# Raising the weight forms' buffers by 192 bytes, and splitting the MLP's plain weight chunks two at a time

## What is computed

```python
D_MODEL = 2048; SEQ = 256; DEPTH = 2; D_FF = 4 * D_MODEL
for l in range(DEPTH):
    ...                                   # mixer: input projection, branches, output projection
    x = layer_norm(ALPHA * x + mix, ln_mix_g[l], ln_mix_b[l])
    h = jnp.square(jax.nn.relu(x @ mlp_w1[l])) @ mlp_w2[l]
    x = layer_norm(ALPHA * x + h, ln_mlp_g[l], ln_mlp_b[l])
```

## Time and profile before

| | |
|---|---|
| median of 3 runs | 2216.68 us (2210.5 to 2217.85) |
| the profiled execution | 2210.79 us, of which the profiled span is 2209.1 us |
| TensorE (matmul) busy | 2187.7 us, 99% of the span |
| TensorE (weight load) busy | 2033.3 us, 92% |
| VectorE busy | 1665.5 us, 75% |
| ScalarE busy | 1152.0 us, 52% |
| chain that ended last | PE 90%, DVE 5%, issue 2%, ACT 2%, DMA 1% |
| mean granted TensorE clock | 0.997 of full speed |
| DMA | 190 GB/s over the span, its main queue 58.7% of 16 engines |

### The profile page before, as it was taken

The page is one execution under the profiler, slowest core; times in us unless marked ns, Lnnn a source line. Parts: engine busy times, 40 slices in busy tenths (PEclk is TensorE's granted clock), DMA queues, the critical chain, the costliest instruction groups (busy, mean ns, idle before and its releaser), DMA issues.

```text
span 2209.1 us, 36685 instructions
## 1 busy us (share of the span) xinstructions
PE 2187.7 (99%) x15395; PEld 2033.3 (92%) x15395; DVE 1665.5 (75%) x1942; ACT 1152.0 (52%) x1244; POOL 48.5 (2%) x77
## 2 busy tenths in 40 slices
PE   9999999999999999999999999999999999999998
PEld 9998988899999999899889999988989989999996
DVE  5999986977787688688765455568777777877786
ACT  5555584455555456466434444444555554555552
POOL 2000010000000000000100000000000000000000
PEclk9999999999999999999999999999999999999999
DMA  7555656555665666566846555564665666656674
GB/s 259 175 161 152 183 161 191 183 179 187 196 200 191 201 196 215 171 192 210 261 139 205 177 172 172 175 206 154 196 194 185 206 191 194 198 188 205 190 230 151
DMA packets 213237, 419.29 MB, mean 190 GB/s; under 512 B 12809, under 2 KB 13377, under 8 KB 212176
## 3 DMA queue, kind: packets, MB, share of 16 engines
q1 hardware_dynamic: 210832, 406.37, 58.7%
q0 software_dynamic: 1952, 10.04, 1.4%
q10 hardware_dynamic: 288, 0.52, 0.1%
HBM read 414.79 MB, written 2.10 MB: 189 GB/s over the span
## 4 chain that ended last, share of the span: by engine, by line
PE 90%; DVE 5%; issue 2%; ACT 2%; DMA 1%; DVEq 0%; SPq 0%; ACTq 0%
PE gemm L1653 13%; PE gemm L1655 13%; PE gemm L1656 13%; PE gemm L1629 12%; PE gemm L1631 12%; PE gemm L1630 11%; PE pair L2077 4%; PE pair L2081 4%; PE pair L2079 4%; DMA raw<-in_mlp_w 1%; PE pair L1810 1%; DVE lnp L1304 1%; DVE w_lo L1012 1%; ACT w_hi L677 1%; DVE w_lo L1482 1%
## 5 line engine op out<-in xcount | busy, mean ns | idle before, releaser
L1012 DVE TENSOR_TENSOR w_lo<-raw,w_hi 128x1024 fp32r<-128x1024 f32 x656 | 787.6, 1226 | 289.7 <-ACT w_hi L677 283.6
L677 ACT ACTIVATE w_hi<-raw 128x1024 fp32r<-128x1024 f32 x656 | 681.8, 1056 | 578.0 <-PE gemm L1656 238.8
L1653 PE MATMUL gemm<-x_hi,w_hi 128*128 128x256 f32 x2912 | 809.0, 278 | 0.2 <-DVE w_lo L1012 0.2
L1655 PE MATMUL gemm<-x_lo,w_hi 128*128 128x256 f32 x2912 | 807.4, 277 | 0.0
L1656 PE MATMUL gemm<-x_hi,w_lo 128*128 128x256 f32 x2912 | 807.2, 277 | 0.0
L1653 PEld LDWEIGHTS gemm<-x_hi,w_hi 128*128 128x128 f32 x2912 | 549.1, 189 | 1.6 <-issue 1.0
L1655 PEld LDWEIGHTS gemm<-x_lo,w_hi 128*128 128x128 f32 x2912 | 548.0, 188 | 0.6
L1656 PEld LDWEIGHTS gemm<-x_hi,w_lo 128*128 128x128 f32 x2912 | 547.5, 188 | 0.0
L1629 PE MATMUL gemm<-w_hi,c_hi 128*128 128x512 f32 x832 | 325.6, 391 | 0.5 <-issue 0.5
L1631 PE MATMUL gemm<-w_hi,c_lo 128*128 128x512 f32 x832 | 324.4, 390 | 0.0
L1630 PE MATMUL gemm<-w_lo,c_hi 128*128 128x512 f32 x832 | 324.2, 390 | 0.0
(11 more groups left out here) (234 smaller groups left out, 2511.0 us busy)
## 6 DMA issues: line engine op xcount, KB each, us to landing
raw<-in_mlp_w SPq DMA_DIRECT2D x512, 512.0 KB, 4.7
raw<-in_ev_w_in SPq DMA_DIRECT2D x96, 512.0 KB, 3.7
raw<-in_od_w_in SPq DMA_DIRECT2D x96, 512.0 KB, 3.8
raw<-in_ev_w_out SPq DMA_DIRECT2D x32, 512.0 KB, 4.5
raw<-in_od_w_out SPq DMA_DIRECT2D x32, 512.0 KB, 4.5
lnp<-in_ln_mix_g POOLq DMA_DIRECT2D x2, 1024.0 KB, 6.4
lnp<-in_ln_mlp_g POOLq DMA_DIRECT2D x2, 1024.0 KB, 6.9
lnp<-in_ln_mlp_b POOLq DMA_DIRECT2D x2, 1024.0 KB, 9.0
```

The lines of the kernel that those rows point to most:

```text
L677: act.activation(hi_of_chunk(s), raw[:, s % RING], ACT.Copy).then_inc(hi_ready, 1)
L1012: dve.tensor_tensor(lo_of_chunk(s), raw[:, s % RING], hi_of_chunk(s).bitcast(F32), ALU.subtract).then_inc(lo_ready, 1)
L1653: pe.matmul(acc[:, m, :], high, hi(k + c), start=begin and m % 2 == 0, stop=False, skip_group_check=True)
L1655: pe.matmul(acc[:, m, :], high, lo(k + c), start=False, stop=False, skip_group_check=True)
```

## The change

The forms in `w_hi2` and `w_lo2` begin 48 elements (192 bytes) above the start of their buffers; the plain chunks that use places 4 to 7 stay where they were. In the MLP the four chunks of a plain unit are no longer rounded and subtracted one by one but in two pairs. One ScalarE instruction covers two chunks after waits for both loads and both places, and raises `hi_ready` by 2 at its end. One VectorE instruction waits for both high parts, both loads and both places, and raises `lo_ready` by 2 at its end. Outside the MLP's unit loop, and in `seven_raw`, nothing changes in the splitting.

```diff
+        BESIDE = 48
...
         def form(buf, f, n=1):
 
-            return buf[:, f * FORM:(f + n) * FORM].rearrange("p (f k n) -> p f k n", f=n, k=CK)
+            return buf[:, BESIDE + f * FORM:BESIDE + (f + n) * FORM].rearrange("p (f k n) -> p f k n", f=n, k=CK)
...
-            return buf[:, FORM:3 * FORM].rearrange("p (k n) -> p k n", k=CK)
+            return buf[:, BESIDE + FORM:BESIDE + 3 * FORM].rearrange("p (k n) -> p k n", k=CK)
...
+        def two_of(lower, upper, s):
+
+            q = PLACE[s]
+            assert PLACE[s + 1] == q + 1 and q % 2 == 0 and s % 2 == 0
+            return lower[:, q:q + 2] if q < RING else upper[:, q - RING:q - RING + 2]
...
+            def split_two(s):
+
+                for c in range(2):
+                    raw_wait(act, s + c)
+                    act.wait_ge(chunk_used, used_before(s + c) + 1)
+                act.activation(two_of(w_hi, w_hi2, s), raw[:, s % RING:s % RING + 2], ACT.Copy).then_inc(hi_ready, 2)
...
-                        for c in range(HALF):
+                        for c in range(0, HALF, 2):
                             if n == 1 and c == 2:
                                 hidden_square(layer, 0, 0)
-                            split(base + UNIT_SLOT[m] + c)
+                            split_two(base + UNIT_SLOT[m] + c)
...
+            def split_two(s):
+
+                dve.wait_ge(hi_ready, s + 2)
+                for c in range(2):
+                    raw_wait(dve, s + c)
+                    dve.wait_ge(chunk_used, used_before(s + c) + 1)
+                dve.tensor_tensor(two_of(w_lo, w_lo2, s), raw[:, s % RING:s % RING + 2],
+                                  two_of(w_hi, w_hi2, s).bitcast(F32), ALU.subtract).then_inc(lo_ready, 2)
...
-                            for c in range(HALF):
-                                split(base + UNIT_SLOT[m] + c)
+                            for c in range(0, HALF, 2):
+                                split_two(base + UNIT_SLOT[m] + c)
```

More of the change, by code:

```diff
@@ L902, in seven_forms @@
                 act.wait_ge(t_ready, seven_no(layer, UNITS[m]))
-                act.activation(seven_hi[:, 3 * FORM:7 * FORM], forms[:, 3 * FORM:7 * FORM], ACT.Copy).then_inc(t_hi, 1)
+                act.activation(seven_hi[:, BESIDE + 3 * FORM:BESIDE + 7 * FORM], forms[:, BESIDE + 3 * FORM:BESIDE + 7 * FORM], ACT.Copy).then_inc(t_hi, 1)
             def mlp(layer):
@@ L1481, in seven_forms @@
                 dve.wait_ge(t_hi, seven_no(layer, UNITS[m]))
-                dve.tensor_tensor(seven_lo[:, 3 * FORM:7 * FORM], forms[:, 3 * FORM:7 * FORM],
-                                  seven_hi[:, 3 * FORM:7 * FORM].bitcast(F32), ALU.subtract).then_inc(t_lo, 1)
+                dve.tensor_tensor(seven_lo[:, BESIDE + 3 * FORM:BESIDE + 7 * FORM], forms[:, BESIDE + 3 * FORM:BESIDE + 7 * FORM],
+                                  seven_hi[:, BESIDE + 3 * FORM:BESIDE + 7 * FORM].bitcast(F32), ALU.subtract).then_inc(t_lo, 1)
             def mlp(layer):
```

## The result

The changed kernel takes 2272.43 us (median of 4, 2264.11 to 2273.55) against 2215.08 us (median of 4) for the kernel before: a ratio of 1.0251, 95% interval 1.0236 to 1.0266. It is slower by 57 us. The direction was forecast; the time lies 9 us above the range.

The account below looks back on a forecast made before the run. TensorE, busy for 99% of the span, was taken as the bound. The terms 10.8 + 2 + 10.8 + 8.8 + 5 - 7.5 gave +30 us on 2210.8, or 2241, with the forecast put at 2243 and the range 2226 to 2263.

Parts of the forecast that it names:

- The bound and the borders: TensorE bounds the kernel; pairs cost time at w2 before w2, w2 before w1, and w1 before w1 then a seven.
- The instruction time: Each pair saves ScalarE 0.19 and VectorE 0.16 us, worth nothing by themselves; VectorE's busy time down by some 30 us.
- the sum: All costs less the shift's gain: 10.8 + 2 + 10.8 + 8.8 + 5 - 7.5 = +30 us on 2210.8.
- w2 before w2 and w2 before w1: At these MLP unit borders TensorE waits 1.8 us for the first pair, 6 times each; 10.8 us per kind.
- w1 before w1: Two w1 units, then a seven: the pair starts the forms' chain 1.1 us later, 8 times, 8.8 us.
- The loads of a pair that leave together: Sevens' loads delayed or sharing bandwidth: 5 us for 13 behind one w1, 2 us for 6 behind two w2.
- The shift: Forms 192 bytes higher speed the sevens' matmuls from 119.5 to 113.4 ns: 14.3 us, of which 7.5 reach the end.
- the rival that it is worth nothing: By the skill page's rule the sevens' address shift gains nothing, so 2243 + 7.5 = 2250 us; chance 0.10.
- The last block: The w2 stall was counted only in blocks 0 to 2, as the last block's w2 units have eight places.
- Rival (a): Stalls wake the clock gate: 3.4 us at half pace behind each of 12, 20 us more, 2263; chance 0.17.
- my own signs of being wrong: TensorE's waits below 15 us, sevens still at 119.5 ns, or half-clock stretches behind the stalls.

Follow-up runs that it names:

- pair_behind_seven: Changed kernel with pairs only for units behind a seven, single splits behind plain units and at each MLP's end; 2207.92 us, ratio 0.9977.
- shift_only: Changed kernel with every plain chunk split singly, the forms still 192 bytes higher; 2211.42 us, ratio 0.999 against the kernel before.

## Why the prediction was right or wrong

**The bound and the borders: right.** All three borders lost time where the steps said. Elsewhere in the blocks' inner part there are two new waits of 0.7 and 1.1 us at or behind a seven, which shorter waits at other sevens make up for, and waits of at most 0.4 us where a `w2` unit needs its second pair.

**The instruction time: put too high.** VectorE's busy time fell by 15 us (1665.5 to 1650.2), not by some 30. The prediction took two single subtracts for 2 x 1.226 = 2.45 us. But singles that follow one another directly overlap: they start 1.14 us apart, and the four from 1049.14 on in the kernel before take 4.63 us together. A pair of 2.29 us saves much less against that. It changed nothing in the sum, where these savings stand at nothing.

**w2 before w2 and w2 before w1: right in kind, 12 x 2.0 instead of 12 x 1.8 us.** The two instructions took what rows 3 said (1.92 and 2.29), and the signals between the engines 0.24 us in place of 0.05: ScalarE started at 549.89, TensorE at 554.34, which leaves 4.45 - 4.21.

**w1 before w1: right.** At six of the eight sevens the start behind the 18th matmul came 1.46 us after the one ahead of it (0.31 before), which is the predicted 1.1 us more. At the first of each MLP it was 1.97 us.

**The loads of a pair that leave together: small.** I put 7 us for 13 sevens behind one `w1` and 6 behind two `w2` units. All waits of sevens grew by 9.4 us, and the `w1` border explains them all (9.8 us at its eight sevens). At the 6 sevens behind two `w2` units no such wait appeared. In pair_behind_seven, which keeps these loads and no border stall, the sevens' waits surpass shift_only's by 2.7 us.

**The shift: the kind was right, the size came out by luck.** I counted 14.3 us of matmul time, at 113.4 ns for every seven, and 7.5 of it reaching the end, since sevens that wait would lose theirs. Both steps were wrong. The sevens gained 8.9 us of matmul time, because many run at 118 ns or change between the two paces. And shift_only shows that the waits didn't take the rest: there the sevens gained 9.5 us, and their waits stayed at 7.4. The two errors nearly cancel. I also held the sevens' pace and the `w1` units' for separate, and only asked whether the `w1` units at 118 ns might be cured; more of them go at that pace now (22 of 60 units, 15 before). In the time of the whole kernel the shift alone is worth 0 to 5 us, and some 7 with the pairs in place. So the rival that it is worth nothing isn't borne out. In "SBUF — State Buffer", section "Who interferes with whom", the Trainium skill lets TensorE wait on nobody; here the time of the same 42 matmuls went from 5.02 to 4.76 us with the address alone. That the cost lies in the reads, as I wrote, no run shows.

**The last block: the step that failed.** I wrote that the last block's units have eight places, and so nothing to lose. That is true of the places and says nothing of the loads. The load of a unit's chunk waits for the subtract of the chunk four before. With pairs the last load of ("w2", 3, 1, 0) left only when the second pair of ("w2", 3, 2, 1) was done. That was 1.7 us behind GpSimd's first load, which starts when the last seven is done, where it had been 2.4 us ahead of it (the whole stretch lies some 21 us later in the changed kernel). So GpSimd's loads stood in front. The sum had no line for GpSimd's queue at all, though its loads stand in the page's part 6. That was 14.5 us.

**The clock: a rival that should have been in the sum.** Rival (a) gave 0.17 to half-clock stretches behind the stalls and at most 20 us. The trace has 9 more of them, and half-clock stretches behind the stalls were among my own signs of being wrong. One, around the border at 728.4 (PE busy first, PEclk after POOL):

```profile
728.00:731.70 3.70, 1.87 (x9) 1.25 (x8) 3.13 (x2) 1.97 (x2) 0.00 (x0) 1.00 0.03 5
731.70:735.10 3.40, 3.40 (x10) 2.62 (x9) 2.11 (x2) 0.63 (x1) 0.00 (x0) 0.50 0.91 321
735.10:738.00 2.90, 2.90 (x14) 2.38 (x14) 2.31 (x3) 1.06 (x1) 0.00 (x0) 1.00 0.99 333
```

TensorE was idle for 1.8 of the first 3.7 us, then the granted clock was 0.50 (1.2 GHz) for 3.4 us. Of the 12 stalls 7 drew such a stretch and 5 didn't, although all are equally long; what tells the seven from the five was not looked into. The two others go with the long waits; the one that begins in the 10.6 us wait is 10.2 us long. Together the half clock took 13.6 us more than before.

So of the 33 us between the sum (30) and the trace (63), 14.5 are the loads behind GpSimd's, 13.6 the clock, and some 5 the `w1` matmuls at 118 ns and the waits at `w2` matmuls, less what I had put too high. Either of the two large ones alone would have left the forecast within its range (2243 + 14.5 or + 13.6); it took both to pass 2263.

## What to carry to other kernels

Before two instructions are merged, look at what the first half's early end let start: a place that was free, a load that left, and what other queue it was ahead of. Merging was free only where the second half's inputs were there about as early as the first's (here behind a seven), and where a buffer's release sets the start it costs what the latency of both engines (4.45 us here) exceeds the work that TensorE still has from that release on (2.44 us here, from 549.89 to the start due at 552.33). Where the sum finds idle stretches on a TensorE that was never idle, half the clock in the 3.4 us behind some of them belongs in the sum and not in a rival.

## What the runs showed of the hardware

At the full granted clock, matmuls of one shape (256 moving columns, each with a weight load of its own) go at one of a few paces: 113.4, 118 or 119.5 to 120 ns. In `w1` units a pace holds for a whole run of 96 or 192 matmuls, and the same buffers can be at 113 in one unit and at 118 in the next. A seven can change its pace on the way. The moving buffer's address bears on which paces occur: the sevens had 119.5 at offset 0, 113 or 118 at 192 bytes, 118 at 64, 118 to 120 at 384.

The pace of one unit goes with that of the unit behind it. In the changed kernel all 12 `w1` units behind a seven that ended at 118 ns ran at 118, and 1 of the 22 behind a seven that ended at 113. In shift_only it was 6 of 6 and 4 of 28. With 64 bytes most `w1` units behind sevens went at 118 ns though their own operands were not moved. Whether the one pace causes the other isn't shown, and the mixers' matmuls ahead of the first seven change their pace from kernel to kernel too. Which rule picks the pace stays open; no run here took the moving and the stationary address apart.

Two loads issued 0.4 us apart by SyncE landed 3.8 and 4.7 us later where nothing else was loading (those of 1058.9 and 1059.3 in the changed kernel), but 11.8 and 17.2 us later when GpSimd's loads (2 MB of them norm parameters) had begun to be issued 1.3 us ahead of the first.
